# Conv FFN of a two-block kernel: down products in PSUM banks 4 to 7, high weight parts cast by ScalarE, low parts shared 1280 : 768

## What is computed

```python
D_FF = 2816
def conv_ffn(hn, w_up, conv_w, conv_b, w_down):
    s = hn.shape[1]
    u, v = jnp.split(hn @ w_up, 2, axis=-1)
    up = jnp.pad(u, ((0, 0), (CONV_WIDTH - 1, 0), (0, 0)))
    uc = conv_b + conv_w[0] * up[:, 0:s]
    for j in range(1, CONV_WIDTH):
        uc = uc + conv_w[j] * up[:, j:j + s]
    return (jax.nn.silu(uc) * v) @ w_down
...
    for layer in range(DEPTH_2):
        ...
        h = h + mix.astype(h.dtype)
        hn = rms_norm(h, ffn_norm_g[layer])
        h = h + conv_ffn(hn, ffn_w_up[layer], ffn_conv_w[layer], ffn_conv_b[layer], ffn_w_down[layer]).astype(h.dtype)
```

## Time and profile before

| | us |
|---|---|
| median of 3 runs | 1981.43 |
| lowest and highest | 1978.73, 1985.42 |
| span of the profiled execution | 1980.1 |
| TensorE, VectorE, GpSimd, ScalarE busy | 1042.3, 1260.4, 870.9, 221.4 |
| network of layer 0, first to last product | 1407.2 to about 1600.5 |
| network of layer 1, first to last product | 1779.9 to about 1973.2 |

### The profile page before, as it was taken

The page is one execution under the profiler, slowest core; times in us unless marked ns, Lnnn a source line. Parts: engine busy times, 40 slices in busy tenths (PEclk is TensorE's granted clock), DMA queues, the critical chain, the costliest instruction groups (busy, mean ns, idle before and its releaser), DMA issues.

```text
span 1980.1 us, 15659 instructions
## 1 busy us (share of the span) xinstructions
PE 1042.3 (53%) x5196; PEld 785.5 (40%) x5196; DVE 1260.4 (64%) x1985; ACT 221.4 (11%) x364; POOL 870.9 (44%) x648
## 2 busy tenths in 40 slices
PE   7999778000000000000000068977899989779998
PEld 6576567000000000000000034465699765349987
DVE  2244238789897989898988921233699421338973
ACT  2223111100000000000000021171100012010000
POOL 3000005777777777777777600000356510015554
PEclk9965789555555555555555589967999999989999
DMA  9330128999998999898999912410363444224534
GB/s 303 115 118 0 48 86 295 341 334 324 329 334 296 341 313 361 289 352 299 356 325 331 355 70 100 170 43 23 118 196 133 170 160 160 85 85 143 196 109 149
DMA packets 162563, 413.52 MB, mean 209 GB/s; under 512 B 11338, under 2 KB 57660, under 8 KB 162369
## 3 DMA queue, kind: packets, MB, share of 16 engines
q0 software_dynamic: 75632, 272.63, 38.6%
q1 hardware_dynamic: 86544, 138.58, 20.6%
q10 hardware_dynamic: 320, 1.43, 0.2%
HBM read 411.55 MB, written 1.05 MB: 208 GB/s over the span
## 4 chain that ended last, share of the span: by engine, by line
PE 48%; issue 20%; DVE 16%; POOL 6%; DMA 6%; ACT 3%; DVEq 0%; POOLq 0%; SPq 0%; ACTq 0%
PE ps L408 16%; PE ps L741 13%; PE ps L752 6%; POOL arena L1682 6%; DMA arena<-in_peer_u,stage 4%; PE ps L417 4%; DVE arena L1381 3%; DVE xT L1404 2%; PE ps L389 1%; PE ps L558 1%; PE ps L580 1%; DMA arena<-in_peer_v,stage 1%; DVE k2tok L1334 1%; DVE k2tok L1327 1%; DVE mixed L1404 1%
## 5 line engine op out<-in xcount | busy, mean ns | idle before, releaser
L1699 POOL TENSOR_TENSOR w_lo<-ring,w_hi 128x1024 fp32r<-128x1024 f32 x66 | 226.7, 3434 | 609.1 <-DVE w_hi L1542 609.1
L389 PE MATMUL ps<-cst,hn 128*128 128x128 f32 x112 | 25.2, 417 | 848.8 <-DVE hn L1054 840.2
L1682 POOL DMA_INDIRECT arena<-in_peer_u,stage x256 | 326.4, 1275 | 110.7 <-issue 64.7
L389 PEld LDWEIGHTS ps<-cst,hn 128*128 128x128 f32 x112 | 22.9, 224 | 852.8 <-DVE hn L1054 839.6
L1381 DVE SCALAR_TENSOR_TENSOR arena<-arena,hn 128x1024 f32<-128x1024 f32 x256 | 306.7, 1224 | 73.4 <-DMA arena<-in_peer_u,stage 66.9
L1682 POOL DMA_INDIRECT arena<-in_peer_v,stage x256 | 277.9, 1085 | 96.3 <-issue 47.2
L408 PE MATMUL ps<-ring,xT 128*128 128x512 f32 (+1 forms) x736 | 314.1, 588 | 5.2 <-ACT xT L813 5.2
L408 PEld LDWEIGHTS ps<-ring,xT 128*128 128x128 f32 x736 | 140.3, 191 | 174.2 <-issue 165.9
L1404 DVE SCALAR_TENSOR_TENSOR mixed<-arena,gatew,mixed 128x1024 f32<-128x1024 f32 x128 | 166.4, 1300 | 10.8 <-DMA arena<-in_peer_v,stage 5.7
L1404 DVE SCALAR_TENSOR_TENSOR xT<-arena,gatew,xT 128x1024 f32<-128x1024 f32 x128 | 166.4, 1300 | 5.5 <-DMA arena<-in_peer_v,stage 5.2
L1542 DVE CAST w_hi<-ring 128x2048 fp32r<-128x2048 f32 x66 | 81.0, 1228 | 77.7 <-PE ps L752 57.0
(11 more groups left out here) (330 smaller groups left out, 1388.1 us busy)
## 6 DMA issues: line engine op xcount, KB each, us to landing
ring<-in_ffn_w_up SPq DMA_DIRECT2D x22, 2048.0 KB, 8.7
ring<-in_ffn_w_down SPq DMA_DIRECT2D x22, 1024.0 KB, 5.0
ring<-in_even_w_in SPq DMA_DIRECT2D x7, 2048.0 KB, 7.6
ring<-in_w_in SPq DMA_DIRECT2D x6, 2048.0 KB, 14.6
ring<-in_odd_w_in SPq DMA_DIRECT2D x6, 2048.0 KB, 7.8
ring<-in_peer_wq SPq DMA_DIRECT2D x4, 2048.0 KB, 8.0
ring<-in_w_out SPq DMA_DIRECT2D x2, 2048.0 KB, 7.7
arena<-in_peer_u,stage POOLq DMA_INDIRECT x256, 6.1
```

Of the source, the lines that this page charges most:

```text
L389: last = nc.tensor.transpose(ps[:, 4 + b, (k % 2) * T + tt * P:(k % 2) * T + (tt + 1) * P], src[:, tt, k * P:(k + 1) * P], ident)
L1682: pool.indirect_dma_start(arena[:, b % GATHER_SLOTS, :], None, table, bass.IndirectOffsetOnAxis(ap=stage[:, half_, k:k + 1], axis=0))\
L1699: nc.gpsimd.tensor_tensor(w_lo[j % 2][:, part], w[:, part], w_hi[j % 2][:, part].bitcast(F32), ALU.subtract).then_inc(lo2_ready, 1)
```

## The change

It has four parts.

1. The down products go to banks 4 to 7, and have a count of their own for being read (`down_read`). The first down product no longer waits for the two up pairs.
2. The cast to `w_hi` moves from VectorE to ScalarE (`cast(j)`), 2048 columns in one Copy, with the waits for the chunk, for unit j - 2, and for both low parts of unit j - 2. In the up part it stands before and behind Silu: cast of unit 2c + 2, Silu of chunk c, cast of unit 2c + 3.
3. The low part is shared as 1280 columns on VectorE and 768 on GpSimd, in place of 1024 and 1024. Both wait for `hi_ready`, which ScalarE now gives.
4. The casts and low parts of a layer's first two units stand between the two residual chunks: on ScalarE behind `chunk_done` of the first, on VectorE between the two adds.

```diff
-        if name.startswith("down") or name == "ple_proj":
+        if name.startswith("down"):
+            plan.append((OWN, tuple(used)))
+        elif name == "ple_proj":
             plan.append((None, tuple(used)))
-            if c == FCH - 1 or name == "ple_proj":
-                used = [used[0] + 1, used[1] + 1]
+            used = [used[0] + 1, used[1] + 1]
...
-                                    last = mm(ps[:, 2 * tt + half_, :], g_[:, 2 * c + k, tt * P:(tt + 1) * P], w[:, k, 512 * half_:512 * half_ + 512],
+                                    last = mm(ps[:, 4 + 2 * tt + half_, :], g_[:, 2 * c + k, tt * P:(tt + 1) * P], w[:, k, 512 * half_:512 * half_ + 512],
...
             def conv_ffn(layer):
-                name = "ffn2" + "ab"[layer]
+                name, j = "ffn2" + "ab"[layer], FUNITS * layer
+                act.wait_ge(chunk_done, CHUNK_AT[("even_w_out", "odd_w_out")[layer]] + 1)
+                cast(j)
+                cast(j + 1)
                 squares(name)
                 root(name, TT)
                 turn(name)
                 for c in range(FCH):
+                    cast(j + 2 * c + 2)
                     act.wait_ge(conv_ready, layer * FCH + c + 1)
                     e = conv[:, c % 2]
                     do(e, e, ACT.Silu).then_inc(conv_silu, 1)
+                    cast(j + 2 * c + 3)
+                for k in range(2 * FCH + 2, FUNITS):
+                    cast(j + k)
+
+            def cast(j):
+
+                i, w = unit_weights(j)
+                act.wait_ge(chunk_loaded[i % RING], 16 * (i // RING + 1))
+                if j >= 2:
+                    act.wait_ge(*unit_free(j))
+                    act.wait_ge(lo_ready, j - 1)
+                    act.wait_ge(lo2_ready, j - 1)
+                do(w_hi[j % 2][:], w, ACT.Copy).then_inc(hi_ready, 1)
...
+                    if c and first_unit is not None:
+                        split(first_unit)
+                        split(first_unit + 1)
                     dve.wait_ge(chunk_done, i1 + c + 1)
...
+            def split(j):
+
+                w = unit_weights(j)[1]
+                dve.wait_ge(hi_ready, j + 1)
+                part = slice(0, LO_CUT)
+                v.tensor_tensor(w_lo[j % 2][:, part], w[:, part], w_hi[j % 2][:, part].bitcast(F32), ALU.subtract).then_inc(lo_ready, 1)
...
-                split(j)
                 norm(name)
-                split(j + 1)
                 turn(name)
...
-                    v.tensor_tensor(h[:, tt, :], h[:, tt, :], pair(tt), ALU.add).then_inc(pair_read[tt], 1)
+                    v.tensor_tensor(h[:, tt, :], h[:, tt, :], psf[:, 2048 + D * tt:2048 + D * (tt + 1)], ALU.add).then_inc(down_read, 1)
...
-                part = slice(FHALF // 2, FHALF)
+                part = slice(LO_CUT, FHALF)
```

More of the change, by code:

```diff
@@ L60 @@
 FUNITS = 3 * FCH
+LO_CUT = 1280
 HQ, HF, HI, HGT, NQ, NKC, NVC, NKS, NVS, NKW, NVW, NGATE, D_IN1 = (
@@ L139 @@
     CHUNK_AT.setdefault(_n, _i)
+OWN = 2
 def bank_plan():
@@ L298, in two_blocks @@
         conv_ready, conv_silu, hidden_ready, x_lo_ready = map(sem, ("conv_ready", "conv_silu", "hidden_ready", "x_lo_ready"))
-        hi_ready, lo_ready, lo2_ready, unit_done = map(sem, ("hi_ready", "lo_ready", "lo2_ready", "unit_done"))
+        hi_ready, lo_ready, lo2_ready, unit_done, down_read = map(sem, ("hi_ready", "lo_ready", "lo2_ready", "unit_done", "down_read"))
         ple_sig, alpha_done, alpha_read, out_stored = map(sem, ("ple_sig", "alpha_done", "alpha_read", "out_stored"))
@@ L333, in unit_weights, with read_out, unit_free @@
             return i, slot(i)[:, lo:lo + FHALF]
-        def read_out(i, side=None):
+        def read_out(i):
             turn_, used = PLAN[i]
-            if turn_ is None:
-                turn_ = side
             return pair_read[turn_], used[turn_] + 1
+        def unit_free(j):
+            before, k = unit_weights(j - 2)[0], (j - 2) % FUNITS
+            if k < 2 * FCH and k % 2 == 0:
+                return unit_done, (j - 2) // FUNITS * FCH + k // 2 + 1
+            return chunk_done, before + 1
         def after(name):
@@ L345, in after @@
                     "mix2a": (h_ready, 2), "ffn2a": read_out(CHUNK_AT["even_w_out"] + 1),
-                    "mix2b": read_out(CHUNK_AT["down0"] + FCH - 1, 1),
+                    "mix2b": (down_read, TT),
                     "ffn2b": read_out(CHUNK_AT["odd_w_out"] + 1),
-                    "end": read_out(CHUNK_AT["down1"] + FCH - 1, 1)}[name]
+                    "end": (down_read, 2 * TT)}[name]
         blockctx = ctx.enter_context(nc.Block())
@@ L1072, in turn, with residual @@
                     ins.then_inc(xT_ready, 1)
-            def residual(name, n=2):
+            def residual(name, first_unit=None):
                 i1 = CHUNK_AT[name]
-                for c in range(n):
+                for c in range(2):
+                    if c and first_unit is not None:
+                        split(first_unit)
+                        split(first_unit + 1)
                     dve.wait_ge(chunk_done, i1 + c + 1)
@@ L1529, in _ @@
             turn("out2")
-            residual("even_w_out")
-            def split(j):
-                i, w = unit_weights(j)
-                dve.wait_ge(chunk_loaded[i % RING], 16 * (i // RING + 1))
-                if j >= 2:
-                    before, k = unit_weights(j - 2)[0], (j - 2) % FUNITS
-                    if k < 2 * FCH and k % 2 == 0:
-                        dve.wait_ge(unit_done, (j - 2) // FUNITS * FCH + k // 2 + 1)
-                    else:
-                        dve.wait_ge(chunk_done, before + 1)
-                v.tensor_copy(w_hi[j % 2][:], w).then_inc(hi_ready, 1)
-                dve.wait_ge(hi_ready, j + 1)
-                part = slice(0, FHALF // 2)
-                v.tensor_tensor(w_lo[j % 2][:, part], w[:, part], w_hi[j % 2][:, part].bitcast(F32), ALU.subtract).then_inc(lo_ready, 1)
+            residual("even_w_out", 0)
             def conv_ffn(layer):
                 name, j = "ffn2" + "ab"[layer], FUNITS * layer
-                split(j)
                 norm(name)
-                split(j + 1)
                 turn(name)
@@ L1621, in _ @@
             turn("out3")
-            residual("odd_w_out")
+            residual("odd_w_out", FUNITS)
             conv_ffn(1)
```

## The result

The changed kernel takes 2019.16 us (median of 4 runs, 2018.51 to 2020.98), the kernel before 1981.86 (4 runs, 1978.73 to 1985.42). The ratio is 1.0164, with a 95% interval of 1.0105 to 1.0222: slower, and outside the predicted range. It is what rival 2 described, at a higher price.

A forecast was written before the change was run, and what follows sets the result against it. TensorE's chain was taken as the bound, with only its two seams able to give time. Each layer gains 7.31 us and loses 5.0, 4.6 us for both, giving 1976.8 us; range 1967.5 to 1984, the forecast's own 1973 to 1981.

The forecast's parts named there:

- rival 2: Up part: GpSimd starts low parts before VectorE, whose loop becomes 13.2 us per chunk; 2005.6 us, slower; chance 0.12.
- Front seam: Ahead of the up products: splitting units between residual adds frees the variance from standing behind GpSimd, gaining 2.13 us per layer.
- Seam to the down part: Between up and down products: banks 4 to 7 remove a 3.48 us gap and 1.70 us of slow matmuls, 5.18 per layer.
- Prices of the steps: New path: ScalarE's cast 1.90 us, VectorE's low part 1.50, GpSimd's work 1.69, both low parts 3.22 behind hi_ready.
- The loop, 5.0 us: Cast, low part, convolution, Silu, next cast take 12.19 us against TensorE's 11.52; new waits total 5.0 us per layer.
- The forecast's 0.5 us in a layer: Allowance for waits queued ahead of a cast and GpSimd's signal to TensorE: 0.5 us, bounds 0 and 2.5.
- a lead of 0.04 us: Low parts after ScalarE's cast: VectorE starts ahead of GpSimd by 0.04 us at most.
- The slack of 0.6 us on VectorE: Up part: VectorE ends its chunk at most 0.6 us before the next even cast; coming later turns the order.

The follow-up runs named there:

- p4_front: Kernel before with only the first two units split between the two residual adds; ratio to before 0.9992.
- p1_banks: Kernel before with only the down products moved to banks 4 to 7; ratio to before 0.9957.
- p14_banks_front: Kernel before with down products in banks 4 to 7 and the first two units split between the residual adds, casts still on VectorE; ratio to before 0.9919.
- e1_one_wait: Changed kernel without VectorE's waits for unit_done and chunk_done ahead of the up part's low parts; ratio to before 0.9996.
- e6_met_wait: Changed kernel with VectorE's unit_done and chunk_done waits replaced by a wait for the first add to h, met long before; ratio to before 1.0162.
- e4_pool_late: Changed kernel with one more, already met wait ahead of GpSimd's subtraction in the up part; ratio to before 1.0001.
- e5_even_only: Changed kernel with only VectorE's unit_done wait at even units taken away, chunk_done kept; 2024.52 us in one run.
- p14_again: p14_banks_front unchanged, measured again; ratio to before 0.9922.
- e3_both: Changed kernel without VectorE's waits ahead of the up part's low parts and with ScalarE's odd-unit cast ahead of Silu; ratio to before 0.9943.

## Why the prediction was wrong, point by point

- **Front seam, 2.13 us: right.** Variance 0.17; 2.32 us less to the first product; p4_front 2.30 in layer 0.
- **Seam to the down part, 5.18 us: right**, 5.07 in layer 1 of p1_banks, and 7.4 for both seams in p14_banks_front (5.6 and 7.4 when measured again). What it missed is the load of down chunk 2, up to 1.9 us, which the old gap had covered.
- **Prices of the steps: right.** ScalarE's cast 1.92 (1.90 taken), VectorE's 1280 columns 1.49 (1.50), GpSimd's 768 columns 3.15 behind VectorE, and 1.85 when it goes first (1.69 of work taken); both low parts are there 3.21 to 3.24 behind the cast in e1_one_wait (3.22). The Trainium skill, page "SBUF — State Buffer", section "Who interferes with whom", says that whoever issues first has the shared pair for its whole length, and that the other blocks. The rows agree, in both directions.
- **The loop, 5.0 us: right in kind for the kernel of e1_one_wait**, where the new waits cost 5.9 and 6.4 us (7.4 of gains less 1.5 and 1.0): 0.8 in every other chunk, 0.96 at unit 23, and 0.1 in each down unit, which the forecast had at 0.03 in every other one. It is wrong for this one. What makes the down units longer was not followed up.
- **The step that failed** is rival 2's dismissal: "GpSimd was the later one at every start that the trace shows". In those starts VectorE's wait was for its own cast, 0.03 us behind it, and nothing else stood between. With the cast gone from VectorE, the waits for `unit_done` and `chunk_done`, which had stood ahead of the cast, stand directly ahead of the low part as a second wait. No line of the diff shows it, since these lines didn't change. The forecast's 0.5 us in a layer was for the waits queued ahead of ScalarE's cast; those ahead of VectorE's low part it did not count at all, nor what they do to a lead of 0.04 us. e1_one_wait and e6_met_wait, which differ in these waits alone, show it: VectorE starts 0.03 us behind the cast with one wait and 0.09 to 0.10 with two, GpSimd 0.07 to 0.08 in both, and the layer takes 17 us more. An honest reading would have said that the lead was unknown, with two waits on one side and one on the other, and made rival 2 at least as likely as the forecast; it had 0.12.
- **Rival 2's size: too small.** It gave 12.1 us in a layer; layer 0 lost 16.0 and layer 1 14.3. Layer 0 set beside p14_banks_front, which has the same seams: from first product to first down product 146.90 us (1411.08 to 1557.98) against 128.16 (1406.28 to 1534.44), 18.7 lost where 17 were priced; from there to the adds 64.81 against 60.11, 4.7 lost where 2.4 were priced. Less 7.3 of gains, 16.1. The loop itself was priced well (13.2, measured 13.3). In the up part the first pattern takes 13.5 us for each chunk, above the 13.2 priced. In the down part 1.7 us are the clock, which I had left out: behind the 2.03 us wait at unit 23 the first 12 matmuls take 4.40 us in place of 2.72. In layer 1 the clock held behind the same wait (2.02 us, then 2.81 for 12 matmuls), and its down part lost 3.4 in place of 4.7. Another 0.8 are the longer down units.
- **The slack of 0.6 us on VectorE** was right (it waits 0.53 to 0.59 us for every other even cast in layer 0 of e4_pool_late) and was named as the other way to lose. e5_even_only shows that it is: there a VectorE held up at the first odd unit is late at the next even one, and the loop stays late.

About 6 us of the difference, ahead of layer 0's stretch, are not explained. 5.7 of them are there when the first block's sum is added to `h` (1146.33 against 1140.65), and in the changed kernel's second profile that add came another 7.8 us later (1154.11), so scatter alone can give this much, and no cause is claimed.

## What to carry to other kernels

Where two engines that exclude each other are released by the same signal, the order of their starts is part of the design: count the waits ahead of each, make the winner have fewer, and price the other order before relying on a lead of a few hundredths of a microsecond. Better still, cut the chain that makes the order matter; here moving one cast ahead of Silu took 20 to 22 us off each layer, with the order of starts as it was. And when a step is moved to another engine, look for what used to stand ahead of it: a wait that was hidden behind the cast now stands ahead of the instruction that has to be first. Test the parts of a change apart: two of the four were worth 14.9 us together (13.0 when measured again), and the other two, as they stood, cost about three times that (22 to 23 us in each layer). With one cast moved they cost 1 to 2 us in a layer. What the share of 1280 to 768 columns is worth by itself no run shows.

## What the runs showed of the hardware

- A second semaphore wait of the up part ahead of a VectorE instruction puts its start at 0.09 to 0.10 us behind the end of ScalarE's cast; with one wait it is 0.03. GpSimd's start with one wait is 0.07 to 0.08. The second wait costs this even if it was met 270 us before (e6_met_wait). GpSimd's start moves in the same way, from there to 0.14 or 0.15 (e4_pool_late).
- VectorE's subtraction (two SBUF inputs) and GpSimd's exclude each other in both directions: 1.49 and 3.15 us when VectorE begins first, 3.17 and 1.85 when GpSimd does, from starts 0.02 to 0.05 us apart.
- TensorE's clock fell behind some waits of 2.0 to 2.3 us and held behind others of the same length. In the changed kernel it was 0.66 in the 5 us behind those that end at 1432.21 and 1459.25 (2.24 us) and 1.00 behind the one that ends at 1486.27 (2.25); at unit 23 it was 0.66 in layer 0 (2.03 us) and 1.00 in layer 1 (2.02). Over the changed kernel, its second profile, e5_even_only and e6_met_wait it fell behind 12 of 17 waits of 2.23 to 2.27 us, behind 4 of 7 of 2.01 to 2.06, and behind none of about 1.5; nor did it behind those of 1.50 and 1.62 in p1_banks and p14_again. What decides between two equal waits no run here shows. It also stood at 0.77 behind the front seam in one layer and at 1.00 in the other of p4_front.
- With the casts on ScalarE a down unit of 24 matmuls takes 5.52 to 5.57 us, with the casts on VectorE 5.44, though TensorE has no idle time of its own ahead of most of them (e3_both against p14_banks_front).
